# A hybrid encoder on one Trainium2 core: weight chunks split in quarters, timed by VectorE's maxima

## The reference, cut to what matters

```python
h = jnp.pad(x @ w_in, ((0, 0), (PAD, 0), (0, 0)))
ya = window_gqa(qa, ka, va, sink) * silu(ga)               # group A: 4 heads, window of 128 and the meta tokens
ob = diff_attention(qb, kb, vb, lam, valid)                # group B: 4 dense heads, two softmaxes each
yb = (rms_norm(ob, subln_w) * (1.0 - lam_init)) * silu(gb)
y_f = hgrn2_chunked(qc, k_f, ic, logf_f)                   # group C: 4 heads, gated recurrence, both directions
y_b = flip(hgrn2_chunked(flip(qc), flip(k_b), flip(ic), flip(logf_b)))
yc = rms_norm(y_f + y_b, c_norm_w) * silu(gc)
return jnp.concatenate([ya, yb, yc], axis=-1)[:, PAD:] @ w_out
```

## Time and profile before

| | us |
|---|---|
| median of 3 runs | 2032.49 |
| lowest and highest of them | 2021.19, 2033.53 |
| the profiled execution | 2035.93 |
| its span in the profile | 2034.6 |
| TensorE matmul busy | 1766.6 (87%) |
| VectorE busy | 1229.3 (60%) |
| ScalarE busy | 885.6 (44%) |
| GpSimd busy | 357.2 (18%), 122 instructions |

### The profile page before, as it was taken

One profiled execution on the slowest core, in us unless ns is written; L12 is line 12 of the kernel. 1 busy time (PEld: TensorE's weight loads), 2 busy tenths in 40 slices (PEclk: granted clock), 3 DMA queues, 4 the chain that ended last, 5 costly groups with the idle time before them and its releaser, 6 DMA issues. The chain is left out here.

```text
span 2034.6 us, 37112 instructions
## 1 busy us (share of the span) xinstructions
PE 1766.6 (87%) x14474; PEld 1645.5 (81%) x14474; DVE 1229.3 (60%) x2793; ACT 885.6 (44%) x2700; POOL 357.2 (18%) x122
## 2 busy tenths in 40 slices
PE   3898999999879897968988989999998798987796
PEld 3888888899778786857988888889988687876696
DVE  7584683455457777874176746834554566767615
ACT  5334434245325564663053344352552254645603
POOL 5410211210120101010343102112102101101024
PEclk9899999999889999989999999999998899998998
DMA  6200100100100000032121001001001000002222
GB/s 240 62 22 11 53 22 26 49 25 12 51 21 7 27 9 26 14 126 91 42 100 58 22 12 53 22 28 47 27 13 46 22 9 27 29 6 101 79 87 83
DMA packets 97132, 91.85 MB, mean 45 GB/s; under 512 B 5120, under 2 KB 87280, under 8 KB 96960
## 3 DMA queue, kind: packets, MB, share of 16 engines
q1 hardware_dynamic: 96960, 89.49, 13.5%
HBM read 68.30 MB, written 21.17 MB: 44 GB/s over the span
## 5 line engine op out<-in xcount | busy, mean ns | idle before, releaser
L771 PE MATMUL psum<-w_hi,hT_hi 128*128 128x256 f32 x2400 | 710.6, 296 | 31.4 <-DVE rb L1661 15.0
L771 PE MATMUL psum<-w_hi,hT_lo 128*128 128x256 f32 x2400 | 688.4, 287 | 0.0
L771 PE MATMUL psum<-w_lo,hT_hi 128*128 128x256 f32 x2400 | 687.3, 286 | 0.0
L771 PEld LDWEIGHTS psum<-w_hi,hT_hi 128*128 128x128 f32 x2400 | 467.4, 195 | 42.5 <-issue 27.1
L771 PEld LDWEIGHTS psum<-w_hi,hT_lo 128*128 128x128 f32 x2400 | 467.1, 195 | 0.0
L771 PEld LDWEIGHTS psum<-w_lo,hT_hi 128*128 128x128 f32 x2400 | 466.3, 194 | 0.0
L739 POOL CAST w_hi<-w_raw 128x2048 fp32r<-128x2048 f32 (+1 forms) x42 | 81.5, 1942 | 1082.4 <-DMA w_raw<-in_w_in 1081.9
L1061 PE MATMUL psum<-vg_b,aT_b 128*128 128x128 f32 (+1 forms) x1224 | 159.4, 283 | 35.7 <-ACT aT_b L1361 35.7
L741 POOL TENSOR_TENSOR w_lo<-w_raw,w_hi 128x2048 fp32r<-128x2048 f32 (+1 forms) x42 | 189.1, 4503 | 3.4
L1800 DVE TENSOR_REDUCE row_max<-psum 128x1 f32<-128x1024 f32 x136 | 165.4, 1216 | 28.3 <-PE psum L912 28.2
L1061 PEld LDWEIGHTS psum<-vg_b,aT_b 128*128 128x128 f32 (+1 forms) x1224 | 146.0, 190 | 43.7 <-ACT aT_b L1361 41.0
(11 more groups left out here) (161 smaller groups left out, 2838.7 us busy)
## 6 DMA issues: line engine op xcount, KB each, us to landing
w_raw<-in_w_in SPq DMA_DIRECT2D x52, 512.0 KB, 4.9
h_dram<-hbuf SPq DMA_DIRECT2D x16, 512.0 KB, 2.6
w_raw<-in_w_out SPq DMA_DIRECT2D x8, 1024.0 KB, 5.1
hbuf<-h_dram SPq DMA_DIRECT2D x16, 512.0 KB, 5.8
qk_b<-y_dram SPq DMA_DIRECT2D x16, 512.0 KB, 3.3
y_dram<-y_stage SPq DMA_DIRECT2D x96, 64.0 KB, 1.6
w_raw<-in_w_in SPq DMA_DIRECT2D x6, 1024.0 KB, 5.4
hbuf<-in_x SPq DMA_DIRECT2D x8, 512.0 KB, 7.5
```

The source lines that it names most:

```text
L771: last = nc.tensor.matmul(out_ap, lhs[a](k), rhs[b](k), start=k == 0 and a + b == 0, stop=k == KT - 1 and b == 1)
```

## The change

Each chunk is loaded in two halves by k-tiles, each with a semaphore of its own, and split in four quarters of two k-tiles: a CAST of 128 x 512 and a TENSOR_TENSOR of 128 x 512 each (in O chunks a multiplication of 128 x 512 ahead of quarters 1 to 3). TensorE waits for a quarter at every second k-tile. For four chunks of a layer the table BESIDE names a dense head: there quarter j of the chunk waits, before its first instruction, until both scores of step j + 1 of that head have been filled, and before its subtraction for the first component's maximum. Chunks B0 vg and B1 vg wait for the end of a C pair's preparation.

```diff
+W_LOADS = 2
+W_PIECES = 4
+PIECE = KT // W_PIECES
+BESIDE = {("B2", "qk"): "B0", ("B3", "qk"): "B1", ("O", 0): "B2", ("O", 1): "B3"}
...
-            at = 0
-            for c0, n in CHUNKS[i][3]:
-                sp.dma_start(w_raw[:, i % 2, :, at:at + n], w[:, :, c0:c0 + n]).then_inc(w_loaded[i % 2], 16)
-                at += n
+            for j in range(W_LOADS):
+                ks = slice(j * KT // W_LOADS, (j + 1) * KT // W_LOADS)
+                at = 0
+                for c0, n in CHUNKS[i][3]:
+                    sp.dma_start(w_raw[:, i % 2, ks, at:at + n], w[:, ks, c0:c0 + n]).then_inc(w_loaded[i % 2][j], 16)
+                    at += n
...
+        def beside_maximum(l, head, n, c):
+            step = b_step(l, head, n, 1)
+            if c == 0:
+                wait_filled(pool, ("s", l, *step, 1))
+            else:
+                pool.wait_ge(b_max, B_COMP[l, *step, 0])
...
+            for j in range(W_PIECES):
+                ks = slice(j * PIECE, (j + 1) * PIECE)
+                raw, hi, lo = (w[:, i % 2, ks, 0:n] for w in (w_raw, w_hi, w_lo))
+                pool.wait_ge(w_loaded[i % 2][j * W_LOADS // W_PIECES], 16 * loads_before(i))
+                if head:
+                    beside_maximum(l, head, j, 0)
+                if g == "O" and j:
+                    pool.wait_ge(norm_w_in, 16)
+                    pool.tensor_tensor(raw, raw, view(norm_w, 0, P, l * 6 + (j - 1) * PIECE, [[1, PIECE], [0, n]]),
+                                       ALU.mult).then_inc(w_scaled, 1)
+                    pool.wait_ge(w_scaled, (W_PIECES - 1) * (l * (DM // CW) + name) + j)
+                pool.tensor_copy(hi, raw).then_inc(w_hi_done, 1)
+                pool.wait_ge(w_hi_done, W_PIECES * i + j + 1)
+                if head:
+                    beside_maximum(l, head, j, 1)
+                pool.tensor_tensor(lo, raw, hi.bitcast(F32), ALU.subtract).then_inc(w_split, 1)
...
+                if name == "vg" and g in ("B0", "B1"):
+                    pool.wait_ge(seg_ready, SEG[l, "C" + g[1], 1, 1])
+                split_chunk(l, g, name, BESIDE.get((g, name)))
...
+        def split_product(out_ap, lhs, rhs, ks, i):
             for k in ks:
+                if k % PIECE == 0:
+                    pe.wait_ge(w_split, W_PIECES * i + k // PIECE + 1)
...
-                pe.wait_ge(w_split, i + 1)
```

More of the change, by code:

```diff
@@ L507, in build @@
     norm_w_in = sem("norm_w_in")
-    w_loaded = [sem(f"w_loaded{i}") for i in range(2)]
+    w_loaded = [[sem(f"w_loaded{i}_{j}") for j in range(W_LOADS)] for i in range(2)]
     w_hi_done = sem("w_hi_done")
@@ L767, in _ @@
     def _(pe):
-        def split_product(out_ap, lhs, rhs, ks=range(KT)):
+        def split_product(out_ap, lhs, rhs, ks, i):
             for k in ks:
+                if k % PIECE == 0:
+                    pe.wait_ge(w_split, W_PIECES * i + k // PIECE + 1)
                 for a, b in ((0, 0), (1, 0), (0, 1)):
@@ L794, in project @@
                     [lambda k, w=w: w[:, i % 2, k, f * P:(f + 1) * P] for w in (w_hi, w_lo)],
-                    [lambda k, h=h: h[:, k * TOK + a:k * TOK + a + n] for h in (hT_hi, hT_lo)], ks)
+                    [lambda k, h=h: h[:, k * TOK + a:k * TOK + a + n] for h in (hT_hi, hT_lo)], ks, i)
             else:
@@ L799, in project @@
                     [lambda k, h=h: h[:, k * TOK + x * P:k * TOK + (x + 1) * P] for h in (hT_hi, hT_lo)],
-                    [lambda k, w=w: w[:, i % 2, k, 0:CW] for w in (w_hi, w_lo)], ks)
+                    [lambda k, w=w: w[:, i % 2, k, 0:CW] for w in (w_hi, w_lo)], ks, i)
             if half != 0:
```

15 lines of the change are left out of this document (1 added, 14 removed).

## The result

| | before | after |
|---|---|---|
| median, us | 2033.01 (4 runs) | 1953.39 (4 runs) |
| lowest and highest | 2021.19, 2033.85 | 1951.07, 1957.13 |
| span of the profiled execution | 2034.6 | 1949.8 |
| mean granted clock of TensorE | 0.948 | 0.966 |

The ratio is 0.9608, with a 95% interval of 0.9577 to 0.9638: 80 us faster. I had forecast 52 (1982 us, in a range from 1955), so the direction and the places were right and the size was too small.

A forecast was written before the change was run, and what follows sets the result against it. VectorE standing still beside GpSimd's instructions, which delays TensorE, was taken as the bound. Gains 30 + 4 + 8 + 3 + 8 - 1 = 52 us off 2035.93 gave 1984, set at 1982 for the median; range 1955 to 2014.

The forecast's parts named there:

- The bound and the mechanism: VectorE instructions on SBUF operands stand still until GpSimd's instruction ends; shorter pieces hold them for less.
- The prices of pieces: For 512 columns on GpSimd: subtraction 1.36 us, CAST 0.62, multiplication about 1.1.
- rival 3: In the heads, a subtraction lasting 2.40 misses its cover: about 2015 to 2025 us, no change; chance 0.05.
- The dense heads: Four chunks beside dense heads lose 7.8 us a layer instead of 23.0: 30 us gained in two layers.
- The price of quarter 0: In B3 qk, O 0 and O 1 it lands after step 1's maxima and runs uncovered: 1.5 us each.
- Half-levels: Four chunks there: 6.6 us held against 6 now, but spread over two half-levels; gain 1 each, 4 in all.
- Group A and rotations with B2 qk: B2 qk loses 0.3 us instead of 4.1; four or five chunks in rotations gain 2 each, 8 in all.
- C0 vg, preparations: Preparations of four pairs gain 2 us each, 8; TensorE's earlier start on C0 vg 1.5 a layer, 3.
- Number 2: Waits gone give back TensorE clock, in gates and rotations too: gain 66 to 82, about 1960 us; chance 0.12.
- Number 1: Outside the heads, turns between GpSimd and VectorE eat the gain: 1995 to 2017, say 2004 us; chance 0.22.

The follow-up runs named there:

- waits_alone: The changed kernel with chunks loaded and split whole, keeping the waits for maxima and for the preparation's end: 2029.11 us, 0.9991 of the kernel before.
- levels_whole: The changed kernel with only C1 qf and B2 vg, the chunks split during half-levels, split whole again: 1960.99 us, 0.9654 of the kernel before.
- whole_ahead: As levels_whole, but the whole chunk's CAST also waits for the scores that start a half-level: 1972.3 us, 0.9691 of the kernel before.
- heads_only: The changed kernel with timed quarters only in B2 qk, B3 qk, O 0, O 1; other 17 chunks whole, no preparation wait: 1992.47 us, 0.9811 of before.
- no_vg_wait: The changed kernel without the wait of B0 vg and B1 vg for the end of a pair's preparation: 1958.47 us, 0.964 of the kernel before.

## Why the prediction was right in kind and wrong in size

**The bound and the mechanism** were right in the main: VectorE stands still beside GpSimd, and short pieces shorten that. Two points differ. The masked copy isn't held, which the prediction had left open. And not every instruction on SBUF operands is held: the reciprocal and the norm's statistics aren't.

**The prices of pieces** were right to 0.05 us. Of the two dearer prices that the prediction weighed, a CAST of 0.77 and halves of C0 vg that land late, neither shows: the CAST takes 0.67, and TensorE's two waits ahead of C0 vg make 2.2 and 2.0 us instead of 4.70, a gain of 2.5 to 2.7 where I had 1.5. Two of the prediction's own figures don't follow from its sums: 52 us off the median is 1980.5, not 1982, and the "22 and more" of rival 3 starts at 2004, not 2015. Neither changes the outcome.

**The dense heads**: 22.8 forecast for three chunks a layer, 30.9 measured for the stage, in which 29.7 us of idle time and 31 us at half clock are gone. From the end of a head's first step to its last, B1 gains 4.1 in both layers (2.5 forecast), B2 6.6 and 5.5 (4.5), B3 4.4 and 4.5 (4.4): 29.2. The other 1.7 is in the first steps of the heads and in B0. The price of quarter 0 was wrong in B1 and B2: 1.5 for a hold of 1.0 that the next step takes up. In O 1 the sum came out.

**Half-levels: the step that failed.** It said: 6.6 held in all against 6 now, gain 1 each, 4 in all. Measured were 4.0 held against 6.05, and 18.6 gained in four passes. That is 14.6 of the 33 us by which the whole gain was forecast too small. Two things are behind it.
- The held time was overcounted, since part of the eight pieces lies under masked copies and costs nothing.
- A loss isn't proportional to what is held. VectorE has 0.7 us of idle time in a half-level. Behind a hold, half-levels follow each other at 3.35 instead of 4.13 (1248.29 to 1251.64 is the line L1667 in after), so 0.8 is regained in each. Five holds of 0.4 to 1.1 over three half-levels nearly vanish in that: 1.0 us over the undisturbed 24.8. Two holds of 1.7 and 4.4 in one half-level don't. They reach TensorE as a wait of 3.4 to 4.0, and its clock falls with it: in this pass it is at half from 1302.75 on for 3.4 us. I had read this loss of 5.0 in the earlier trace rows, and then compared only the sums of holds, as if the wait of TensorE and the clock would stay.

TensorE's own rows show it. Before, in C1 of layer 1, and beside it 35 us of the same pass after, by engines (x counts, then PEclk):

```profile
1302.98 2.08 PE L847 MATMUL psum<-qk,k_sel 64*128 64x128 f32 x16 [3.40 <-ACT k_sel L1217]
```

```profile
1290.00:1325.00 35.00, 31.60 (x295) 29.51 (x293) 29.61 (x45) 11.87 (x35) 7.03 (x2) 0.95 0.06 19
```

```profile
1225.00:1260.00 35.00, 34.25 (x337) 32.00 (x336) 30.82 (x53) 14.18 (x41) 8.46 (x8) 1.00 0.11 32
```

After, TensorE gets through 337 matmuls in 35 us instead of 295, at full clock instead of 0.95. (The second stretch lies earlier in its pass. From 1288.21 and 1233.20, with the chunk in the first 8 us of both, it is 294 and 333.) In the four passes together 10.8 us of idle time and all 20.2 us at half clock are gone. Half of 20.2 is 10.1, and both make 20.9 against 18.6 measured.

The clock's part can be seen by itself. The C1 pass with a half-level of 9.43 us (a whole chunk's long one) occurs five times, with more or less half clock in it. It takes 57.7 us with none (waits_alone, layer 1), 59.3 with 3.4, 60.8 with 6.6 and again with 6.7, and 61.8 with 9.2: 0.45 to 0.47 us for each microsecond at half. Of the 24 passes with a whole chunk, 14 have a TensorE wait of 3.40 to 4.00 us, and in 13 of them the clock fell to half between 0.8 us ahead of its end and 1.3 behind it. The other ten have a longest wait of 1.71 to 2.08, and it fell there in two. Why it falls behind one wait and not behind the like one isn't settled.

How much of the 18.6 is the pieces' size and how much their place? Put back whole there, chunks lengthen the passes by 7.3 us in one placement (levels_whole, about 9 in the total) and by 12.3 in another (whole_ahead, about 16 in the total by the two ratios, 0.9691 and 0.9611, with more time at half clock outside the passes). Sixteen whole chunks were split in passes without a wait for VectorE (in before, waits_alone, heads_only and levels_whole). Eleven began 0.01 to 0.56 us into a half-level, and that half-level took 9.43 or 9.87. Five began 0.60 to 0.97 into one, and it took 7.92 to 7.96. All four of before were of the first kind. With quarters no pass lost as much, wherever the first one fell (55.3 to 56.3 us). Even the 7.3 of levels_whole has one long pass in it. The shortest passes that any kernel had with a whole chunk are 56.9 and 56.9 in C0, 56.7 and 56.5 in C1, 3.7 over after in all. So where a whole chunk falls well, quarters win only these 3.7 of the 18.6; the other 14.9 come, with the wait and the clock behind them, from a place that before hit four times in four, and that quarters make harmless.

**Group A and rotations with B2 qk**: 15.6 forecast, 23.8 measured. heads_only has B2 qk's part and what follows from it, 13.3, where I had 7.6. The other chunks bring 10.5 where I had 8. Here 9.8 us of TensorE's idle time and 20 us at half clock are gone, the latter outside my terms of held instructions. The idle time and half of the other make 19.8 of the 23.8. The remaining 4 I can't place.

**C0 vg, preparations**: 10 forecast, 11.8 measured in the gates, preparations, the stretches between and the tail together. C0's two preparations got longer, by 4.6 and 4.0 us, where I had a gain of 2 each. In layer 0 the moved B0 vg explains 3.5 of it (no_vg_wait has 12.5 there). In layer 1 it doesn't, and the cause stays open.

**The rivals.** Number 2, a gain of 66 to 82 through clock given back, gave the number that came out, and I had it at 0.12. Over the whole span TensorE's idle time fell from 252 to 193 us, and the time in which it was busy at half clock from 165.7 to 107.2. 59 and half of 58.5 make 89 against the 85 gained. So about a third of the gain is clock and two thirds are waits. That this count is sound shows in all 17 traces: TensorE's busy time less half of what it was busy at half clock is 1683.8 to 1689.6 us in each, though the spans go from 1947 to 2038. Number 1 is refuted: small pieces hold VectorE in turns, as forecast, and that helps. Number 3 fell with the price of 1.31. The rule of the Trainium skill (SBUF — State Buffer, Who interferes with whom), that whichever starts first keeps the shared ports for its whole instruction, agrees with the rows here, 4.60 beside 4.92 as much as 1.24 beside 1.35.

## What to carry to other kernels

Shorten the pieces of the engine that blocks before timing them: untimed quarters brought 69 of 80 us. Timing beside the maxima brought 12 against untimed quarters of halved loads, and nothing without the size; untimed quarters of whole loads came within 2 us of it in the heads. Try the cheap version first. Choose the size by the slack of the blocked engine between two of its deadlines, and stop where the pieces' own start-up makes the data late (two subtractions of 256 columns take 1.61 us where one of 512 takes 1.31, by the means of after). When a hold is priced, don't add up the held time. Compare each hold with the slack: under it a hold costs little, over it the wait goes on to the next engine, and there it can also cost clock. Check first where the blocking instruction begins: moving a whole one by half a microsecond was worth 3 to 5 us a pass here.
